# One block-triangular inverse in a chunked scan: 128-row products on the full TensorE array against 64-row block products, with the products grouped by array shape

## The chip, the cores and the metric

The kernel runs on one core of a Trainium2 chip. The metric is the device time of one execution in microseconds (us), here the median of three runs. Beside the time there is one profiled execution; its trace records each instruction of TensorE (matmuls as PE, weight loads as PEld), VectorE (DVE), ScalarE (ACT), GpSimd (POOL) and the DMA queues. Durations below are us unless marked otherwise.

## The reference

Two model blocks run one after another over 1024 tokens of width 1024. The part that the change touches most is the scan of the first block, a delta-rule recurrence over 16 heads of width 64, once forward and once backward:

```python
def rwkv7_scan(r, w, k, v, kk, a, S0, reverse):
    ...
    def step(S, inp):
        w_t, k_t, v_t, kk_t, b_t = inp[:5]
        sa = jnp.einsum('bhvk,bhk->bhv', S, kk_t)
        S = (S * w_t[:, :, None, :] - sa[..., None] * b_t[:, :, None, :]
             + v_t[..., None] * k_t[:, :, None, :])
        o = jnp.einsum('bhvk,bhk->bhv', S, inp[5]) if with_out else None
        return S, o
```

The outputs of both directions are added, normalized per head, scaled and shifted, a bonus is added and the sum is multiplied by a gate. The second block has differential attention with four heads of width 128, beside it a gated linear recurrence; their eight 128-row results are concatenated and multiplied by `w_out`:

```python
attn = rms_norm_2(attn, subln_w[l]) * (1.0 - lambda_init)
...
x = x + jnp.concatenate([attn, y], axis=-1) @ w_out[l]
```

## The kernel before

**The scan's units.** `rwkv` (line 923) cuts the 1280 tokens (256 of context, 1024 of the sequence) into ten tiles of 128. A unit is one pair of heads `i` (8 of them) and one pair of tiles `n` (5; `n` = 0 is the context, which has no output), so there are 40. In each unit both directions are done, set `x` = 0 forward and `x` = 1 backward, and each set holds four 128 x 128 problems `q` (two heads, two tiles). All work is written out by hand, one order for each engine; the engines meet by semaphores that the class `Marks` counts. In the table of names, `F` marks belong to the front of a unit (worked on during the unit before it), `L` marks to its levels, `B` marks to its back.

**The inverse.** With a chunk of 128 tokens the recurrence becomes a triangular system, (I + A) Y = R. Its inverse is built by doubling: `Y0` holds the inverses of the 2 x 2 diagonal blocks, and each level m = 1 to 6 doubles the size of the blocks. A level has three products of four 128 x 128 x 128 matmuls per set, written by the helper `quad`: `g` makes G from `Mr` and X into PSUM bank 0, VectorE (`join`) multiplies it by a mask `lev{m}` into SBUF; `x_next` makes the new X from Y and G in bank 1, `y_next` the new Y from G and Y in bank 2, and ScalarE (`x_out`, `y_out`) copies both to SBUF. `levels` (line 1280) gives TensorE's order: g of set 0, y of set 1 of the level before, g of set 1, x and y of set 0, x of set 1. Operands are of type fp32r; those of the rest of the scan are fp32, where each matmul stands twice in the trace. Each set has four PSUM banks of its own.

**The rest of a unit.** After the levels TensorE turns the next unit's keys and values (`turn_kv`, `turn_ab`), interleaved with the last y of both sets; `solve` multiplies the inverse by the right-hand sides `Rr`, `product` and `refine` do one step of refinement. Between them stand `gram_b` and `gram_k` of the next unit, products of 64 rows with the head's two halves h = 0, 1 in the two row halves of the array. `passing` makes the matrices that carry the state over a tile; `start` of the next unit transposes `Y0` to X (line 1244) and makes `MakV` (line 1247); at last `state` (line 1328) makes for each tile k and set x the new state (lines 1344, 1346, 1348) and, for n > 0, the output (lines 1353, 1355, 1357). Of these, 1344, 1346, 1353 and 1355 use all 128 rows and one column half; 1348 and 1357 are the 64 x 64 products with the carried state `S`.

```python
for x in range(2):
    if nxt:
        gram_b(*nxt, x)
    product(i, n, x)
refine(i, n, 0)
if nxt:
    gram_k(*nxt, 0)
    gram_k(*nxt, 1)
refine(i, n, 1)
for x in range(2):
    passing(i, n, x)
    if nxt:
        start(*nxt, x)
for k in range(2):
    for x in range(2):
        state(i, n, x, k)
```

**The tail.** Each pair's output is normalized by steps that sit between levels of the next pair's units: `center`, `spread`, `normal`, `affine` on VectorE, `square` and `finish` (bonus, gate) on GpSimd, `tail` (Ln, Exp) on ScalarE. For the last pair they stand alone after the last unit, and the next stage, `retention`, starts when all engines are through.

**Attention and what follows.** `attend` (line 2408) writes each head's result from `out` to the DRAM tensor `cat` by GpSimd's queue and waits for the stores at its end. `ring` is a pair of weight buffers in SBUF; `attend` loads the first two chunks of `w_out` into them. `out_up` reads `cat` back by SP's queue into `raw`, two buffers, in the order k = 0 to 3, splits each into a high and a low part (`cut.hi` on ScalarE, `cut.lo` on VectorE), loads `xb` (4 MB) on the same queue and multiplies. For the first chunk TensorE goes k by k.

Of the kernel before, what the change touches and what calls it, by code (L numbers as in the profile page):

```python
# [16 lines left out]
F32R = mybir.dt.float32r  # L17
# [846 lines left out]
class Marks:  # L864
# [23 lines left out]
    def wait(self, eng, i, name):  # L888
# [6 lines left out]
     "row", "rest"] + [f"lev{m}" for m in range(7)])}  # L895


def constants():
# [8 lines left out]
    for m in range(7):  # L907
        t[f"lev{m}"] = 1.0 * (p == f) - 1.0 * ((p >> (m + 1) == f >> (m + 1)) & (p >> m != f >> m))
# [14 lines left out]
def rwkv(nc, G, proj, Xd, oa, v_tok, rope):  # L923
# [15 lines left out]
    with nc.cleanup_on_exit(), ExitStack() as ctx:  # L939
# [23 lines left out]
        X = [sb(f"X{x}", [P, 4, P], F32R) for x in range(2)]  # L963
        Y0 = [sb(f"Y0{x}", [P, 4, P], F32R) for x in range(2)]
        Y = [sb(f"Y{x}", [P, 4, P], F32R) for x in range(2)]
        Gs = [sb(f"G{x}", [P, 4, P], F32R) for x in range(2)]
# [13 lines left out]
        spare = lambda h: bank(h, 3)  # L980

# [4 lines left out]
        def front_names(n):  # L986
            xs = n > 0
            return {"pe": ["T1", "T0", "gB", "gK", "XT", "MakV"], "act": ["Ktok", "Vtok", "Atok", "Btok", "X0", "AMv"],
                    "dve": ["tri", "MrbT", "MakT", "MrkT"] if xs else ["tri", "MakT"], "pool": ["Y0", "Mr", "AMr"]}

        def level_names(n):
            xy = sum(([f"X{m}", f"Y{m}"] if m < last else [f"Y{m}"] for m in lev), [])
            return {"pe": sum(([f"G{m}", f"X{m}", f"Y{m}"] if m < last else [f"G{m}", f"Y{m}"] for m in lev), []),
                    "act": xy, "dve": [f"G{m}" for m in lev]}
# [26 lines left out]
        with nc.Block() as block:  # L1021
            @block.sync
            def _(sp):
# [20 lines left out]
                def store(i):  # L1044
                    pool_t.wait(sp, i, "o4")
                    sp.dma_start(oa[i], o[i % 2][:]).then_inc(stored, 16)
                load(0)
# [11 lines left out]
                store(HP - 1)  # L1059
                sp.wait_ge(stored, 16 * HP)  # L1060

            @block.gpsimd
            def _(pool):
                tt, ts = nc.gpsimd.tensor_tensor, nc.gpsimd.tensor_scalar

                def front(i, n):
                    e = par_of(i, n)
                    for x in range(2):
                        F[x]["dve"].wait(pool, i, f"{n}.tri")
                        F[x]["pool"].done(tt(Y0[x][:], tri[x][e][:], rep(K("lev0"), 4), ALU.mult), f"{n}.Y0")  # L1070
# [17 lines left out]
                pool.wait_ge(set_up, 8)  # L1088
# [8 lines left out]
                square(HP - 1)  # L1097
                finish(HP - 1)

            @block.scalar  # L1100
            def _(act):
# [20 lines left out]
                def start_out(i, n, x):  # L1122
                    e = par_of(i, n)
                    F[x]["pe"].wait(act, i, f"{n}.XT")
                    F[x]["act"].done(A(X[x][:], heads(x, 1), ACT.Copy), f"{n}.X0")
                    F[x]["pe"].wait(act, i, f"{n}.MakV")
                    F[x]["act"].done(A(AM[x][e][:, :, 1], bank(x, 0)[:, 0:256].rearrange("p (q c) -> p q c", q=4), ACT.Copy), f"{n}.AMv")

                def x_out(i, n, x, m):
                    L[x]["pe"].wait(act, i, f"{n}.X{m}")  # L1130
                    L[x]["act"].done(A(X[x][:], heads(x, 1), ACT.Copy), f"{n}.X{m}")  # L1131

                def y_out(i, n, x, m):
                    L[x]["pe"].wait(act, i, f"{n}.Y{m}")
                    L[x]["act"].done(A(Y[x][:], heads(x, 2), ACT.Copy), f"{n}.Y{m}")  # L1135
# [15 lines left out]
                for i, n in UNITS_B:  # L1151
# [18 lines left out]
                    if n in (1, 2):  # L1170
                        for x in range(2):
                            out(i, n, x)
                tail(HP - 1)

            @block.tensor
            def _(pe):
# [62 lines left out]
                def start(i, n, x):  # L1239
# [3 lines left out]
                    for q in range(4):  # L1243
                        mm = mmul(bank(x, 1)[:, q * P:(q + 1) * P], Y0[x][:, q], ident_r[:], start=True, stop=True)
                    F[x]["pe"].done(mm, f"{n}.XT")
                    for q in range(4):
                        mm = mmul(bank(x, 0)[:, q * 64:(q + 1) * 64], MakT[x][:, q], KV[x][e][:, 1, q], start=True, stop=True)
# [7 lines left out]

                def g(i, n, x, m):
# [5 lines left out]
                    L[x]["pe"].done(quad(bank(x, 0), Mr[x], X[x]), f"{n}.G{m}")  # L1262

                def x_next(i, n, x, m):
# [3 lines left out]
                    L[x]["pe"].done(quad(bank(x, 1), Y0[x] if m == 1 else Y[x], Gs[x]), f"{n}.X{m}")  # L1268

                def y_next(i, n, x, m):  # L1270
                    i_, n_ = before(i, n)
                    if m == 1 and i_ >= 0:
                        B[x]["dve"].wait(pe, i_, f"{n_}.S1" if n_ < 4 else f"{n_}.S0")
# [3 lines left out]
                    L[x]["pe"].done(quad(bank(x, 2), Gs[x], Y0[x] if m == 1 else Y[x]), f"{n}.Y{m}")  # L1277
# [50 lines left out]
                def state(i, n, x, k):  # L1328
                    e = par_of(i, n)
                    t = TILES[x][2 * n + k] - at(x, n)  # L1330
                    s = (2 * n + k) % 2
                    half = lambda h: slice(64 * h, 64 * h + 64)
# [1967 lines left out]
```

## Time and profile before

| | |
|---|---|
| runs | 4991.71, 4992.29, 4998.8 us; median 4992.29 |
| the profiled execution | 4996.18 us, its span 4994.4 |
| TensorE, matmuls | 4816.6 us (96% of the span), 28888 |
| TensorE, weight loads | 3877.0 us (78%) |
| VectorE | 2559.7 us (51%) |
| ScalarE | 1870.5 us (37%) |
| GpSimd | 437.3 us (9%) |
| the scan's units | from 1387 to 2862 us of the span |
| mean granted clock of TensorE | 0.977 |

The span runs from the first to the last instruction of the trace. The time of matmuls is the union of their records, each of which holds the latency of the array as well as its own columns, so a busy PE is not yet a full one; the starts of matmuls and weight loads show the pace. A granted clock of 1.00 is 2.4 GHz, 0.50 is 1.2 GHz.

### The profile page before, as it was taken

How to read it: one execution, taken by the hardware profiler on the slowest of the kernel's cores; microseconds unless marked ns; L12 is line 12 of the kernel's file. 1: busy time of each engine (PE TensorE's matmuls, PEld its weight loads, DVE VectorE, ACT ScalarE, POOL GpSimd, SP SyncE). 2: the span in 40 equal slices, each digit the busy share in tenths (PEclk: the TensorE clock that was granted, in tenths of full speed). 3: DMA queues.
4: the chain of work that ended last, by engine and by line, in shares of the span. 5: the costliest groups of instructions: out<-in, count | busy, mean ns of one | idle time of the engine just before them, and what ended most of it. 6: DMA issues, size and time to landing. Idle time of an engine off the chain costs nothing. (4 is left out here: it accounts for less than half of the span.)

```text
span 4994.4 us, 68841 instructions
## 1 busy us (share of the span) xinstructions
PE 4816.6 (96%) x28888; PEld 3877.0 (78%) x28888; DVE 2559.7 (51%) x3696; ACT 1870.5 (37%) x3155; POOL 437.3 (9%) x352
## 2 busy tenths in 40 slices
PE   8999999999999999999999969899999879999999
PEld 5888877878988888888888734478778557888887
DVE  3344554546344554554555467554543655555553
ACT  3244434444244544545455433421233653111111
POOL 0000000000022232222322200000000000000000
PEclk9999999999989999999999989999999889999999
DMA  5333343434311011011010144242220021122222
GB/s 198 120 137 138 143 146 139 144 139 161 106 71 47 14 59 46 14 59 46 22 51 1 43 130 159 96 156 96 90 80 29 27 85 62 74 76 72 85 102 93
DMA packets 149506, 444.02 MB, mean 89 GB/s; under 512 B 16448, under 2 KB 46400, under 8 KB 131920
## 3 DMA queue, kind: packets, MB, share of 16 engines
q1 hardware_dynamic: 133856, 385.03, 21.7%
q0 software_dynamic: 9584, 33.63, 1.9%
q10 hardware_dynamic: 5760, 20.97, 1.1%
q8 instruction: 230, 3.77, 0.3%
q14 instruction: 76, 0.62, 0.0%
HBM read 295.91 MB, written 142.61 MB: 88 GB/s over the span
## 5 line engine op out<-in xcount | busy, mean ns | idle before, releaser
L172 PE MATMUL pr_ps<-uhl,w_split 128*128 128x512 f32 (+1 forms) x1520 | 586.2, 386 | 3.1 <-DVE w_split L144 2.2
L176 PE MATMUL pr_ps<-uhl,w_split 128*128 128x512 f32 (+1 forms) x1520 | 571.1, 376 | 0.0
L175 PE MATMUL pr_ps<-uhl,w_split 128*128 128x512 f32 (+1 forms) x1520 | 570.6, 375 | 0.0
L1452 DVE TENSOR_TENSOR b_G<-b_ps,cst 128x512 fp32r<-128x512 f32 x480 | 328.3, 691 | 336.5 <-PE b_ps L1253 335.2
L137 ACT ACTIVATE w_split<-share 128x2048 fp32r<-128x2048 f32 x64 | 122.6, 1915 | 689.3 <-DVE ou_vc L3128 270.8
L172 PEld LDWEIGHTS pr_ps<-uhl,w_split 128*128 128x128 f32 x1520 | 286.7, 189 | 81.6 <-issue 29.2
L1131 ACT ACTIVATE b_X<-b_ps 128x512 fp32r<-128x512 f32 x400 | 240.2, 600 | 242.5 <-PE b_ps L1253 242.5
L175 PEld LDWEIGHTS pr_ps<-uhl,w_split 128*128 128x128 f32 x1520 | 286.9, 189 | 56.0 <-issue 5.8
L176 PEld LDWEIGHTS pr_ps<-uhl,w_split 128*128 128x128 f32 x1520 | 286.5, 189 | 52.7
L1253 PE MATMUL b_ps<-b_G,b_Y 128*128 128x128 f32 x1920 | 313.6, 286 | 13.3 <-DVE b_G L1452 13.2
L1135 ACT ACTIVATE b_Y<-b_ps 128x512 fp32r<-128x512 f32 x480 | 286.6, 597 | 88.5 <-PE b_ps L1253 88.5
L1253 PE MATMUL b_ps<-b_X,b_Mr 128*128 128x128 f32 x1920 | 305.2, 286 | 0.0
L1253 PE MATMUL b_ps<-b_Y,b_G 128*128 128x128 f32 x1920 | 300.7, 280 | 0.3 <-DVE b_G L1452 0.3
L172 PE MATMUL ou_ps<-ou_a,w_split 128*128 128x512 f32 x704 | 276.4, 393 | 14.5 <-DVE ou_a L1995 14.5
L1253 PEld LDWEIGHTS b_ps<-b_G,b_Y 128*128 128x128 f32 x1920 | 255.5, 193 | 33.0 <-DVE b_G L1452 18.6
L1070 POOL TENSOR_TENSOR b_Y<-b_tri,cst 128x512 fp32r<-128x512 f32 x80 | 101.9, 1274 | 2034.0 <-DVE b_tri L1439 2034.0
L175 PE MATMUL ou_ps<-ou_a,w_split 128*128 128x512 f32 x704 | 274.6, 390 | 0.0
L176 PE MATMUL ou_ps<-ou_a,w_split 128*128 128x512 f32 x704 | 274.5, 390 | 0.0
L172 PE MATMUL mx_ps<-mx_a,w_split 128*128 128x512 f32 x640 | 258.3, 404 | 16.3 <-DVE w_split L156 16.3
L1253 PEld LDWEIGHTS b_ps<-b_X,b_Mr 128*128 128x128 f32 x1920 | 254.5, 194 | 13.5 <-issue 12.0
L1253 PEld LDWEIGHTS b_ps<-b_Y,b_G 128*128 128x128 f32 x1920 | 258.2, 195 | 0.4 <-DVE b_G L1452 0.4
L745 DVE COPY pr_stage<-pr_ps 128x256 f32<-128x256 f32 (+1 forms) x92 | 49.7, 540 | 401.8 <-PE pr_ps L176 401.7
(470 smaller groups left out, 10284.8 us busy)
## 6 DMA issues: line engine op xcount, KB each, us to landing
w_ring<-in_w_in SPq DMA_DIRECT2D x41, 1024.0 KB, 5.2
proj<-pr_stage SPq DMA_DIRECT2D x160, 256.0 KB, 2.0
share<-in_w_up SPq DMA_DIRECT2D x24, 1024.0 KB, 4.7
ar<-share SPq DMA_DIRECT2D x32, 512.0 KB, 2.8
b_AR<-ar SPq DMA_DIRECT2D x16, 1024.0 KB, 11.9
pr_raw<-proj SPq DMA_DIRECT2D x48, 256.5 KB, 3.4
ada<-in_ada_w SPq DMA_DIRECT2D x24, 512.0 KB, 5.7
ff<-ou_vc ACTq DMA_DIRECT2D x24, 512.0 KB, 2.6
```

The source lines that it names most:

```text
L137: self.nc.scalar.activation(self.hl[:, n % NBUF, 0], raw, ACT.Copy).then_inc(self.hi_done, 1)
L172: mm = nc.tensor.matmul(dst, a[0], b[0], start=start, stop=False)
L175: nc.tensor.matmul(dst, a[0], b[1], start=False, stop=False)
L176: return nc.tensor.matmul(dst, a[1], b[0], start=False, stop=stop)
L745: V.tensor_copy(dst, src).then_inc(taken[1], 1)
L1070: F[x]["pool"].done(tt(Y0[x][:], tri[x][e][:], rep(K("lev0"), 4), ALU.mult), f"{n}.Y0")
L1131: L[x]["act"].done(A(X[x][:], heads(x, 1), ACT.Copy), f"{n}.X{m}")
L1135: L[x]["act"].done(A(Y[x][:], heads(x, 2), ACT.Copy), f"{n}.Y{m}")
L1253: mm = mmul(bk[:, q * P:(q + 1) * P], lhsT[:, q], rhs[:, q], start=True, stop=True)
L1452: L[x]["dve"].done(V.tensor_tensor(Gs[x][:], heads(x, 0), rep(K(f"lev{m}"), 4), ALU.mult), f"{n}.G{m}")
```

## The change

**Levels.** Levels 1 to 5 never mix the two 64-row halves of a chunk, so they are now done on the two diagonal 64 x 64 blocks alone. Each product becomes eight matmuls with 64 rows, 64 columns of weights and 64 moved columns, alternately in the lower and the upper row half of the array; all results lie on partitions 0 to 63, block 0 in one PSUM bank and block 1 in another. ScalarE and VectorE take each result in two instructions of 64 partitions x 256 elements, which write partitions 0 to 63 and 64 to 127. G and X now share banks 0 and 1 of a set, and the y results of both sets share the two banks 2, so y of one set waits until the other's was copied. The sixth level makes only the off-diagonal corner: four matmuls for g, four for y, one eviction each. The transposes of `Y0` in `start` become block products too, and GpSimd makes `Y0` in two halves with a wait between them.

```diff
+                def blocks(at_, lhsT, rhs):
+                    for q in range(4):
+                        for b in range(2):
+                            mm = mmul(at_(b)[:, q], lhsT(b)[:, q], rhs(b)[:, q], start=True, stop=True)
+                    return mm
...
-                    L[x]["pe"].done(quad(bank(x, 0), Mr[x], X[x]), f"{n}.G{m}")
+                    if m < last:
+                        mm = blocks(lambda b: g_at(x, b), lambda b: Mr[x][rows(b), :, rows(b)], lambda b: X[x][rows(b)])
+                    else:
+                        mm = corner(g_at(x, 0), Mr[x][rows(src[x]), :, rows(dst[x])], X[x][rows(src[x])])
+                    L[x]["pe"].done(mm, f"{n}.G{m}")
...
+                    if x == 1 and m < last:
+                        L[0]["act"].wait(pe, i, f"{n}.Y{m}")
+                    if x == 0 and m > 1:
+                        L[1]["act"].wait(pe, i, f"{n}.Y{m - 1}")
...
                 def x_out(i, n, x, m):
                     L[x]["pe"].wait(act, i, f"{n}.X{m}")
-                    L[x]["act"].done(A(X[x][:], heads(x, 1), ACT.Copy), f"{n}.X{m}")
+                    for b, name in enumerate((f"X{m}a", f"X{m}")):
+                        L[x]["act"].done(A(X[x][rows(b)], x_at(x, b), ACT.Copy), f"{n}.{name}")
...
                     L[x]["pe"].wait(dve, i, f"{n}.G{m}")
-                    L[x]["dve"].done(V.tensor_tensor(Gs[x][:], heads(x, 0), rep(K(f"lev{m}"), 4), ALU.mult), f"{n}.G{m}")
+                    if m == last:
+                        L[x]["dve"].done(V.tensor_scalar(Gb[x][rows(dst[x])], g_at(x, 0), -1.0, None, ALU.mult), f"{n}.G{m}")
+                    else:
+                        for b, name in enumerate((f"G{m}a", f"G{m}")):
+                            L[x]["dve"].done(V.tensor_tensor(Gb[x][rows(b)], g_at(x, b), rep(K(f"lev{m}")[0:64, 0:64], 4), ALU.mult), f"{n}.{name}")
```

**Order.** The products of a kind stand together: both `gram_b`, both `product`, both `gram_k`, both `refine`, both `start`, both `passing`. `state` is cut in four, and for each tile all local products come first, then those with the carried state. VectorE's masks follow in the same order. The first local product also waits for the next unit's `AMv`, since `MakV` now goes to bank 2.

```diff
+                    if nxt:
+                        gram_b(*nxt, 0)
+                        gram_b(*nxt, 1)
+                    product(i, n, 0)
+                    product(i, n, 1)
                     if nxt:
                         gram_k(*nxt, 0)
                         gram_k(*nxt, 1)
+                    refine(i, n, 0)
                     refine(i, n, 1)
+                    if nxt:
+                        start(*nxt, 0)
+                        start(*nxt, 1)
+                    passing(i, n, 0)
+                    passing(i, n, 1)
                     for k in range(2):
-                        for x in range(2):
-                            state(i, n, x, k)
+                        states(i, n, k)
...
+                def states(i, n, k):
+                    for step, needed in ((state_local, passes(n, k)), (out_local, n), (state_carried, passes(n, k)), (out_carried, n)):
+                        if needed:
+                            for x in range(2):
+                                step(i, n, x, k)
```

**The last pair's tail.** Its square goes from GpSimd to ScalarE, its scale, shift, bonus and gate to VectorE, the gate in two halves that are stored one by one.

**After attention.** `out` now lies in the second buffer of `ring`. Heads 0 and 1 are stored to `cat` as before; heads 2 and 3 stay in SBUF, where `out_up` reads them first. The second chunk of `w_out` can therefore be loaded only later.

```diff
-                for k in range(HK):
-                    if k >= 2:
-                        cut.wait(sp, k - 1)
+                for k in range(2):
                     sp.dma_start(raw[:, k % 2], cat[:, k]).then_inc(raw_in[k % 2], 16)
                 sp.dma_start(xb[:], x2).then_inc(init_in, 16)
+                cut.wait(sp, 2)
+                ring.load(sp, w_o[1], 0, 0, 1, split=True)
...
+        kept, ORDER = heads_kept(ring), [2, 3, 0, 1]
```

## Rows read from the trace of the kernel before

**Rows 1.** The page, costliest groups: busy us, mean ns, idle before, releaser.
```profile
L1452 DVE TENSOR_TENSOR b_G<-b_ps,cst 128x512 fp32r<-128x512 f32 x480 | 328.3, 691 | 336.5 <-PE b_ps L1253 335.2
```

**Rows 2.** Windows; per engine busy us (count), granted clock, DMA share, GB/s.
```profile
1730.22:1745.80 15.58, 15.24 (x130) 15.01 (x128) 7.94 (x12) 10.57 (x20) 0.00 (x0) 1.00 0.00 1
1712.05:1723.84 11.79, 11.79 (x98) 9.54 (x97) 8.82 (x18) 3.02 (x7) 6.92 (x5) 1.00 0.00 1
1723.84:1730.22 6.38, 6.38 (x97) 4.47 (x96) 1.46 (x5) 0.38 (x1) 1.49 (x1) 1.00 0.01 3
...
2850.00:2852.00 2.00, 2.00 (x11) 2.00 (x11) 0.69 (x1) 1.55 (x2) 0.00 (x0) 0.50 0.00 0
...
1386.00:1414.60 28.60, 28.60 (x136) 28.48 (x135) 7.61 (x11) 12.59 (x22) 3.25 (x3) 0.50 0.37 152
```

**Rows 3.** Order of time, one level: start, us, engine, line, out<-in, count.
```profile
1736.84 0.62 PE L1253 MATMUL b_ps<-b_X,b_Mr 128*128 128x128 f32 x4
1737.34 0.66 PE L1253 MATMUL b_ps<-b_G,b_Y 128*128 128x128 f32 x4
...
1739.67 0.66 PE L1253 MATMUL b_ps<-b_X,b_Mr 128*128 128x128 f32 x4
```

**Rows 4.** Order of time, first X of a unit whose first G starts at 1730.22.
```profile
1731.67 0.66 PE L1253 MATMUL b_ps<-b_G,b_Y 128*128 128x128 f32 x4 [0.34 <-DVE b_G L1452]
```

**Rows 5.** Order of time, both `gram_k` with the next product, in two units.
```profile
1716.75 2.00 PE L1226 MATMUL b_ps<-b_AR,b_Kt 64*128 64x256 f32 x16
...
1718.68 0.66 PE L1253 MATMUL b_ps<-b_G,b_Y 128*128 128x128 f32 x4
...
1753.48 0.97 PEld L1226 LDWEIGHTS b_ps<-share 64*128 64x128 f32 x16
...
1754.57 0.52 PEld L1253 LDWEIGHTS b_ps<-b_G,b_Y 128*128 128x128 f32 x4
```

**Rows 6.** Order of time, state products of one tile and set, TensorE alone.
```profile
1723.84 0.34 PE L1344 MATMUL b_ps<-b_KV 128*64 128x64 f32 x4
...
1724.00 0.29 PE L1346 MATMUL b_ps<-b_WN,b_MB 128*64 128x64 f32 x4
...
1724.22 0.33 PE L1348 MATMUL b_ps<-b_S,b_QT 64*64 64x64 f32 x4
...
1724.48 0.44 PE L1353 MATMUL b_ps<-b_MrkT,b_KV 128*64 128x128 f32 x4
...
1724.75 0.39 PE L1355 MATMUL b_ps<-b_MB,b_WN 128*64 128x128 f32 x4
```

**Rows 7.** Order of time, two 256-element instructions in a row, ScalarE and VectorE.
```profile
1711.26 0.42 ACT L1119 ACTIVATE b_AM<-b_ps 128x256 f32<-128x256 f32 x1
1711.53 0.43 ACT L1120 ACTIVATE b_MB<-b_ps 128x256 f32<-128x256 f32 x1
...
1717.21 0.41 DVE L1460 TENSOR_TENSOR b_WN<-b_C,b_ps 128x256 f32<-128x256 f32 x1
1717.54 0.41 DVE L1461 SCALAR_TENSOR_TENSOR b_WN<-b_ps,b_C 128x256 f32<-128x256 f32 x1
...
1721.66 0.38 ACT L1127 ACTIVATE b_AM<-b_ps 128x256 f32<-128x256 f32 x1 [0.29 <-PE b_ps L1247]
```

**Rows 8.** Order of time, finish of the last pair; one of two GpSimd steps.
```profile
2875.51 1.23 DVE L1422 TENSOR_TENSOR b_o<-b_o,b_osq 128x1024 f32<-128x1024 f32 x1 [3.49 <-ACT b_osq L1108]
...
2877.67 2.34 POOL L1085 TENSOR_TENSOR b_o<-b_o,b_bonv 128x1024 f32<-128x1024 f32 x1 [10.58 <-DVE b_o L1427]
```

**Rows 9.** Order of time after attention; last row: landing of xb's load.
```profile
4085.16 0.53 POOL L2466 DMA_DIRECT2D cat_d<-at_out  x1 [7.39 <-ACT at_out L2601]
...
4089.63 1.91 ACT L153 ACTIVATE w_split<-share 128x2048 fp32r<-128x2048 f32 x1 [4.76 <-PEq L2416]
...
4095.56 0.76 PE L172 MATMUL ou_ps<-ou_a,w_split 128*128 128x512 f32 x1 [11.99 <-DVE ou_a L1995]
...
DMA to landing us min/median/max: 14.8/14.8/14.8
```

More of the change, by code:

```diff
@@ L894 @@
     ["ident", "ident64", "heads64", "after", "from", "before", "upto", "chunk", "rot", "ahead", "behind", "up", "down",
-     "row", "rest"] + [f"lev{m}" for m in range(7)])}
+     "row", "rest"] + [f"lev{m}" for m in range(6)])}
 def constants():
@@ L1172, in _ @@
                             out(i, n, x)
+                dve_t.wait(act, HP - 1, "omu")
+                pool_t.done(A(osq[:], o[(HP - 1) % 2][:], ACT.Square), "osq")
                 tail(HP - 1)
@@ L1272, in y_next @@
                     if m == 1 and i_ >= 0:
-                        B[x]["dve"].wait(pe, i_, f"{n_}.S1" if n_ < 4 else f"{n_}.S0")
+                        for z in range(2):
+                            B[z]["dve"].wait(pe, i_, f"{n_}.S1" if n_ < 4 else f"{n_}.S0")
                     if m == last:
@@ L1326, in passing @@
                     B[x]["pe"].done(mm, f"{n}.GQ")
[L1328 to L1332, printed above, removed]
+                half = lambda h: slice(64 * h, 64 * h + 64)
+                tile = lambda n, x, k: TILES[x][2 * n + k] - at(x, n)
+                passes = lambda n, k: not (n == 4 and k == 1)
+                z_of = lambda n, x, k, h: bank(x, 2)[half(h), tile(n, x, k) * 64:tile(n, x, k) * 64 + 64]
@@ new lines, in state_carried, with out_carried @@
+                def state_carried(i, n, x, k):
+                    s = (2 * n + k) % 2
+                    B[x]["dve"].wait(pe, i, f"{n}.QT")
+                    if k == 0 and n == 0:
+                        pe.wait_ge(s_zero[x], i + 1)
+                    for h in range(2):
+                        mm = mmul(z_of(n, x, k, h), QT[x][half(h), tile(n, x, k)], S[x][half(h), s], start=False, stop=True)
+                    B[x]["pe"].done(mm, f"{n}.Z{k}")
+                def out_carried(i, n, x, k):
+                    s = (2 * n + k) % 2
+                    if not passes(n, k):
+                        B[x]["dve"].wait(pe, i, f"{n}.S0")
+                    for h in range(2):
+                        mm = mmul(o_of(n, x, k, h), S[x][half(h), s], GT[x][half(h), tile(n, x, k)], start=False, stop=True)
+                    B[x]["pe"].done(mm, f"{n}.O{k}")
@@ L2453, in _ @@
                 sp.dma_start(wg[:, 1], w_x).then_inc(w_in, 16)
-                for g in range(2):
-                    ring.load(sp, w_next[g], 0, 0, g, split=True)
+                ring.load(sp, w_next[0], 0, 0, 0, split=True)
                 for k in range(RT):
```

177 lines of the change are left out of this document (106 added, 71 removed).

## The prediction

> **What bounds the kernel now.** I read the page first: TensorE is busy nearly all the time, and VectorE's most costly group in the scan idles as long as it works, always for TensorE [rows 1]. Then the table of windows over one unit (one step of the 40 in the scan, here with outputs): its levels take 15.58 us, with weight loads busy for 15.01 of them; the stretch from the first gram to the state products takes 11.79, the state products 6.38 [rows 2]. Then the order of time. In a level each of six products of four matmuls starts 0.44 to 0.50 after the one before it, and the level comes back after 2.83 us (1736.84 to 1739.67) [rows 3]: 6 x 0.44 = 2.64 and two short pauses, so TensorE sets the levels. Only the first level waits for VectorE, 1.45 us from the first G to the first X [rows 4]. Outside the levels TensorE is fed as well, but it loses time where the array's shape changes: sixteen 64-row matmuls of 256 columns cost 0.107 each (1.71) and the next 128-row one starts after 1.93, so 0.22 for the change [rows 5]. Among the state products, of the same size, it is 0.16 from one group of four to the next without a change, and 0.22 to 0.27 with one [rows 6].
>
> **The block products.** G, X and Y of levels 1 to 5 become eight matmuls of 64 rows, 64 columns of weights and 64 moved columns. No row shows them. Bounds for a product: below, the halves overlap fully, four pairs of 0.04 = 0.16; above, each costs half of a full one, 8 x 0.055 = 0.44, no gain. Between them lie groups of four 64-column matmuls, 0.16 or 0.04 each [rows 6], and the grams' weight loads: sixteen 128-column loads in the two row halves, 1.09 with the change, so about 0.06 each where a full one needs 0.11, while the 256-column matmuls ran one after another [rows 5]. I take 0.04 each, p = 0.32, the nearest row. It is complete to the waiting engine about 0.56 after its start (7 x 0.04, 0.24 for the last, as in 0.33 for four [rows 6], and 0.04).
>
> The Trainium skill, TensorEngine Tiling (Array Packing), section Key Properties, says that different tiles load weights and multiply in parallel. The grams agree for the loads and not for the multiplications (0.107 for 256 columns, in different halves); by the page p would be 0.16, which is the second rival.
>
> **The evictions double in number.** Each is now two instructions of 256 elements on 64 partitions. ScalarE starts two such 0.27 apart, and one lasts 0.38 to 0.42 [rows 7]: a pair occupies 0.54 and is seen 0.70 after its start. VectorE: 0.33 apart, 0.41 long [rows 7], 0.80 with the semaphore.
>
> The Trainium skill, VectorE: DVE Perf Modes, section Two Vector instructions with no wait between them, says that an instruction whose output starts in another quadrant than the last one's starts only when all earlier ones are finished; the halves of G write partitions 0 and 64. No row here shows such a pair. By that rule VectorE's pair would be 0.88, and the period below 2.70 in place of 2.66, or 6 us more in all.
>
> **The new level.** With TensorE at 6 x 0.32 = 1.92 and ScalarE at 4 x 0.54 = 2.16, neither is full; a ring of waits sets the pace. ScalarE takes X0, Y0, X1, Y1 in that order, so X1 starts 1.08 after X0 and is seen 0.70 later; then g of the second set issues, 0.32, and behind it in TensorE's queue the next x of the first, complete after 0.56: 1.78 + 0.32 + 0.56 = 2.66. The other ring, X0, g, VectorE, x, is 0.70 + 0.56 + 0.80 + 0.56 = 2.62. The new waits for shared banks (y of one set on the other's Y) are met inside this: y1 waits until 1.24 after X0's start, before g1 at 1.78; x behind y0 was not due. So 2.66 against 2.83, and what is late next is ScalarE's fourth-in-line X1. Stage: first X after 1.45 (0.56 + 0.80 + 0.09; now 1.45 too), four periods 10.64, then 0.56 + 1.78 and 0.16 for the corner's g: 14.6 against 15.58, so 1.0 saved. Bounds: p = 0.44 gives a period of 2.90 and a stage 0.3 longer than now; p = 0.16 gives 2.34 and 2.6 saved.
>
> **Last level and turn.** Sixth G and Y shrink from 0.44 to 0.16 each, but five changes of shape appear around the transposes (0.7), and the wait of the second solve (0.2) goes. Net 0, give or take 0.4.
>
> **Grams to passing.** Eleven changes of shape cost 1.95 in the row of 11.79 and the 0.15 ahead of it; the new order has nine at 0.13 to 0.22, 1.48. The start's four full transposes become eight block matmuls, twice 0.12 less. Saved 0.7. I followed VectorE's queue through the new order: its fourteen steps of about 0.6 end some 8 us after the first gram, passing starts at 9.3, so nothing is late. GpSimd's Y0 in two halves with a wait between is the same work, done 1.3 before the second start asks for it.
>
> **State products.** Per tile pair now 8 changes; then two. By the gaps of [rows 6] a pair of sets falls from 3.19 to 2.74. A chunk's VectorE step (seen 0.7 after the carried product) is covered by 0.96 of other products where there are outputs, so 0.95 saved in three of five units, 0.65 in the last; at n = 0, without outputs, the cover is gone and nothing is saved. Mean 0.7. The added wait, on the next unit's AMv ahead of the first local product, has all state products queued behind it; ScalarE has AMv about 0.4 to 0.8 before TensorE is through passing, so it costs nothing; were it late by one eviction, 0.4 a unit, 16 in all.
>
> **Sum.** 1.0 + 0 + 0.7 + 0.7 = 2.4 per unit, 96 us in 40. Against it: the 28 tail steps of 0.8 to 1.3 on VectorE sat in its idle half; the new gap in a level is 0.8, so each pushes the ring by some 0.4, -10. For it: the first unit ran at the lower clock (0.50, 1.2 GHz), its levels took 28.60 [rows 2]; at that clock a ring in place of full loads is about 18, 10 less where a usual unit is 1.0 less, +9. The last pair's finish leaves GpSimd: two steps of 2.34 become two halves of VectorE, together as its 1.23, less a wider step before: +3 [rows 8]. In the second block the stage after attention no longer waits for the last head's store: it issues at 4085.16 and the next stage begins at 4089.63; of 4.5 I take 3, since the split of the weights still starts the products [rows 9]. The load of the second weight chunk moves behind xb, which takes 14.8 to land [rows 9]; products start at 4095.56 and need the chunk some 23 us later, so it stays hidden by about 4; if not, 4 to 6 us are lost. Other parts of that edit (two cat loads less) cost nothing, as TensorE never waited for them. Together 101.
>
> The profiled execution took 4996.18 with a span of 4994.4; the median is 4992.29. I subtract from the median: 4891.
>
> **Rivals.**
> 1. *ScalarE does its halves one after another* (output in the other half of the partitions): a pair is 2 x 0.38 and seen after 0.81, X1 starts 1.52 after X0, period 1.52 + 0.81 + 0.32 + 0.56 = 3.21, stage 17.5 against 15.58. With 1.4 saved elsewhere a unit loses 0.5; all in all 4997, 4975 to 5040 over p. For it: nothing here shows ScalarE changing partitions. Against it: the 0.27 held between different tiles.
> 2. *The row halves overlap in the array*, p = 0.16: four rings of 2.34, 4.0 saved per unit: 4825. Against it the grams.
> 3. *The clock falls in the levels*, the slower case. Every wait there becomes part of each level. After pauses of 0.2 to 0.4 in the last unit the clock was 0.50 at 2850 to 2852 [rows 2]. At 1.2 GHz p is about 0.6, the ring 3.4, the levels 3.5 longer and 2.5 more until the clock returns behind them, as in the first unit: 6 per unit, 240 in all, 5130. It turns the result round if more than four in ten units are hit. Against it: the states, of just such small matmuls, ran at 1.00 [rows 2].
> 4. *The change doesn't do what it says*: products at p = 0.44. The levels gain nothing, the order's 1.4 stays: 4941. It is in the forecast's range.
>
> **How the numbers follow.** Forecast 0.50 (4850 to 4945), rival 2 0.13, rival 1 0.25 (0.06 faster, 0.08 same, 0.11 slower), rival 3 0.07, a smaller gain of 10 to 50 us 0.05. The measurement tells about 0.2%, 10 us, from no change. Faster 0.74, same 0.08, slower 0.18. For eight in ten the range reaches from inside rival 2 to most of rival 1: 4835 to 5015.
>
> **What would show it.** Level period 2.66; block products at 0.32; ScalarE's halves 0.27 apart (0.38: rival 1); changes of shape; states 5.4 in place of 6.38; the clock at 1.00 all through the levels; no wait for w_split in the last stage. It would be wrong at its root if ScalarE became full in the levels.

## The result, and the profile after

| | before | changed | ratio, 95% interval |
|---|---|---|---|
| time, us (median) | 4994.0 | 5214.7 | 1.044 (1.042 to 1.046) |
| span of the profiled execution | 4994.4 | 5212.8 | |
| the scan's units in it | 1386 to 2862 | 1387 to 3097 | |
| mean granted clock, whole span | 0.977 | 0.885 | |

Both kernels were timed beside each other, four executions each. The kernel became 221 us slower; forecast was 4891, range 4835 to 5015. The loss lies in the scan, which takes 1710 us in place of 1476; the rest of the kernel is some 15 us shorter. The first thing to look at is the line of the page with the granted clock, in 40 slices of the span of the changed kernel. Slices 11 to 24 hold the scan; before, its slices were all 9 but one.

```profile
PEclk8999999999867677676776769999999989999999
```

The windows of the changed kernel say the same in us (stretch, then busy us and count for TensorE, its loads, VectorE, ScalarE and GpSimd, then the granted clock, the DMA share and GB/s):

```profile
1387.00:3097.00 1710.00, 1573.65 (x18617) 1327.60 (x18618) 774.11 (x1780) 902.94 (x2370) 394.20 (x338) 0.70 0.09 33
...
1716.90:1734.00 17.10, 15.36 (x236) 13.09 (x235) 9.87 (x24) 5.24 (x15) 6.46 (x6) 1.00 0.01 1
1734.00:1757.90 23.90, 22.47 (x236) 19.45 (x238) 7.03 (x17) 17.00 (x46) 0.00 (x0) 0.50 0.01 2
1757.90:1774.90 17.00, 15.86 (x232) 13.51 (x228) 11.67 (x28) 2.90 (x8) 8.79 (x8) 1.00 0.01 2
1774.90:1802.20 27.30, 25.53 (x271) 22.39 (x268) 8.97 (x20) 18.67 (x51) 1.83 (x3) 0.50 0.00 1
...
1767.60:1772.20 4.60, 4.60 (x100) 3.86 (x94) 1.71 (x8) 0.00 (x0) 0.78 (x1) 1.00 0.01 4
```

In every unit of some 43 us (37 before) the clock falls to 0.50 soon after the levels begin (a unit's first G is at 1729.67 and at 1772.20) and in most units comes back only 24 to 27 us later, well behind them (in one of five 20 us): the turn, the solve and a gram run at half clock too. Where before 0.50 stood in the scan at its two ends alone [rows 2], it now stands in 1010 us of it. The last row is the state products: 4.60 in place of 6.38 [rows 2], and at 1.00.

On the page, the group that answers to [rows 1], and the two of ScalarE beside it:

```profile
L1529 DVE TENSOR_TENSOR b_Gb<-b_ps,cst 64x256 fp32r<-64x256 f32 x800 | 333.2, 417 | 310.3 <-PE b_ps L1283 296.3
...
L1147 ACT ACTIVATE b_X<-b_ps 64x256 fp32r<-64x256 f32 x800 | 301.5, 377 | 233.3 <-PE b_ps L1283 218.1
...
L1156 ACT ACTIVATE b_Yb<-b_ps 64x256 fp32r<-64x256 f32 x640 | 241.3, 377 | 41.2 <-PE b_ps L1283 25.5
```

And a level of the changed kernel in order of time, at half clock (start, us, engine, line; compare [rows 3]):

```profile
1779.37 0.78 ACT L1147 ACTIVATE b_X<-b_ps 64x256 fp32r<-64x256 f32 x2
...
1780.17 0.78 ACT L1156 ACTIVATE b_Yb<-b_ps 64x256 fp32r<-64x256 f32 x2
1780.20 0.64 PE L1283 MATMUL b_ps<-b_X,b_Mr 64*64 64x64 f32 x8 [0.17 <-ACT b_X L1147]
1780.65 0.61 PE L1283 MATMUL b_ps<-b_Gb,b_Yb 64*64 64x64 f32 x8
...
1780.88 0.87 DVE L1529 TENSOR_TENSOR b_Gb<-b_ps,cst 64x256 fp32r<-64x256 f32 x2 [0.66 <-PE b_ps L1283]
...
1781.31 0.78 ACT L1147 ACTIVATE b_X<-b_ps 64x256 fp32r<-64x256 f32 x2 [0.36 <-PE b_ps L1283]
...
1782.92 0.78 ACT L1147 ACTIVATE b_X<-b_ps 64x256 fp32r<-64x256 f32 x2
...
1783.75 0.64 PE L1283 MATMUL b_ps<-b_X,b_Mr 64*64 64x64 f32 x8 [0.17 <-ACT b_X L1147]
```

The G at 1780.20 has waited for the second set's X, evicted from 1779.37; the one after it in the same place is at 1783.75, so a level takes 3.55 (2.83 before). Its ring: two pairs of halves on ScalarE at 0.80 each (1781.31 to 1782.92: 1.61), seen after 0.83, G 0.45, X complete 0.66: 3.55. Two things are new in it. A pair of halves on ScalarE takes 0.80, not 0.54, and one on VectorE 0.87. And at half clock a block product occupies TensorE for 0.45.

At full clock a block product is cheaper than forecast. Sixteen matmuls (two products) take 0.65 with the last one's end and eight take 0.42, so a product occupies TensorE for 0.23:

```profile
1772.20 0.65 PE L1283 MATMUL b_ps<-b_X,b_Mr 64*64 64x64 f32 x16
...
1773.76 0.42 PE L1283 MATMUL b_ps<-b_Gb,b_Y 64*64 64x64 f32 x8 [0.90 <-DVE b_Gb L1529]
...
1774.22 0.78 ACT L1147 ACTIVATE b_X<-b_ps 64x256 fp32r<-64x256 f32 x2 [7.47 <-PE b_ps L1283]
```

X is complete to ScalarE after 0.46. From the second set's X to the G that waits for it there are 0.83 at full clock as well:

```profile
1733.13 0.78 ACT L1147 ACTIVATE b_X<-b_ps 64x256 fp32r<-64x256 f32 x2
...
1733.96 0.64 PE L1283 MATMUL b_ps<-b_X,b_Mr 64*64 64x64 f32 x8 [0.29 <-ACT b_X L1147]
```

So at full clock the ring would be 1.60 + 0.83 + 0.23 + 0.46 = 3.12, in place of 2.66 as forecast. That is an estimate from these rows.

### The profile page after: what moved, and what is told of

The parts are those of the page before. It is cut to its first block and busy times, and to the rows that moved or that the text cites. A ratio compares the mean times of both kernels' runs of the same rounds, so it can differ in the third digit from the quotient of the medians.

```text
span 5212.8 us, 80517 instructions
## 1 busy us (share of the span) xinstructions
PE 4927.2 (95%) x34008; PEld 3917.0 (75%) x34008; DVE 2595.6 (50%) x4100; ACT 2043.0 (39%) x4036; POOL 444.3 (9%) x427
## 5 line engine op out<-in xcount | busy, mean ns | idle before, releaser
L1529 DVE TENSOR_TENSOR b_Gb<-b_ps,cst 64x256 fp32r<-64x256 f32 x800 | 333.2, 417 | 310.3 <-PE b_ps L1283 296.3
L1147 ACT ACTIVATE b_X<-b_ps 64x256 fp32r<-64x256 f32 x800 | 301.5, 377 | 233.3 <-PE b_ps L1283 218.1
L1085 POOL TENSOR_TENSOR b_Y<-b_tri,cst 64x256 fp32r<-64x256 f32 x160 | 115.7, 723 | 2270.2 <-DVE b_tri L1512 2264.0
L172 PE MATMUL mx_ps<-mx_a,w_split 128*128 128x512 f32 x640 | 259.3, 405 | 15.8 <-DVE w_split L156 15.8
L1156 ACT ACTIVATE b_Yb<-b_ps 64x256 fp32r<-64x256 f32 x640 | 241.3, 377 | 41.2 <-PE b_ps L1283 25.5
L175 PE MATMUL mx_ps<-mx_a,w_split 128*128 128x512 f32 x640 | 254.1, 397 | 0.0
L176 PE MATMUL mx_ps<-mx_a,w_split 128*128 128x512 f32 x640 | 254.0, 397 | 0.0
L1283 PE MATMUL b_ps<-b_X,b_Mr 64*64 64x64 f32 x3200 | 213.2, 269 | 27.0 <-ACT b_X L1147 26.3
L651 ACT ACTIVATE pr_stage<-pr_ps 128x256 f32<-128x256 f32 (+1 forms) x92 | 43.9, 477 | 484.8 <-PE pr_ps L176 480.9
L1283 PEld LDWEIGHTS b_ps<-b_X,b_Mr 64*64 64x64 f32 x3200 | 174.2, 187 | 69.3 <-ACT b_X L1147 46.2
L175 PE MATMUL ou_ps<-ou_ext,w_split 128*128 128x512 f32 x576 | 224.1, 389 | 0.0
```

The costliest lines, as they stand in the source:

```text
L172: mm = nc.tensor.matmul(dst, a[0], b[0], start=start, stop=False)
L175: nc.tensor.matmul(dst, a[0], b[1], start=False, stop=False)
L176: return nc.tensor.matmul(dst, a[1], b[0], start=False, stop=stop)
L651: A(dst, src, ACT.Copy).then_inc(taken[0], 1)
L1085: F[x]["pool"].done(tt(Y0[x][rows(b)], tri[x][e][rows(b), :, rows(b)], rep(K("lev0")[rows(b), 0:64], 4), ALU.mult), f"{n}.{name}")
L1147: L[x]["act"].done(A(X[x][rows(b)], x_at(x, b), ACT.Copy), f"{n}.{name}")
```

## The experiments

Two theories stood against each other from the start: the half clock makes the loss (rival 3), or the halved evictions make it by themselves (rival 1). Times of before beside the runs are 4994 to 4997; intervals of the ratios are 0.0009 to 0.002 wide on either side. e9 and e12 are medians of two executions, the others of four or more.

| run | what it is | us | ratio to before | clock, 1700 to 2000 |
|---|---|---|---|---|
| e1 | levels as before, all else changed | 4903.9 | 0.982 | 1.00 |
| e2 | + one matmul nobody needs per product | 5224.5 | 1.046 | 1.00 |
| e3 | two passes, one eviction per product | 4916.8 | 0.985 | 1.00 |
| e4 | two passes, evictions in halves | 5066.7 | 1.015 | 1.00 |
| e5 | Y three times, single pass | 5382.9 | 1.078 | 0.72 |
| e6 | the same, Y's halves swapped | 5387.8 | 1.079 | 0.70 |
| e7 | X in two passes, one eviction | 4980.0 | 0.997 | 0.97 |
| e8 | X and G so | 4910.1 | 0.983 | 0.99 |
| e9 | each product twice, single pass | 5413.2 | 1.084 | 0.70 |
| e10 | e4, Y's halves swapped | 5024.1 | 1.006 | 1.00 |
| e11 | before, with the edit after attention | 4986.7 | 0.998 | |
| e12 | each product three times, single pass | 5279.7 | 1.057 | 0.94 |

**e1: the levels back, the rest kept.** `blocks` and `corner` are `quad` again, X, Y and G are evicted whole.

```
-                        mm = blocks(lambda b: g_at(x, b), lambda b: Mr[x][rows(b), :, rows(b)], lambda b: X[x][rows(b)])
...
+                    L[x]["pe"].done(quad(bank(x, 0), Mr[x], X[x]), f"{n}.G{m}")
...
-                    for b, name in enumerate((f"X{m}a", f"X{m}")):
-                        L[x]["act"].done(A(X[x][rows(b)], x_at(x, b), ACT.Copy), f"{n}.{name}")
+                    L[x]["act"].done(A(X[x][:], heads(x, 1), ACT.Copy), f"{n}.X{m}")
```

> The changed kernel with its five levels (and the sixth, and the start's transposes) put back to products of all 128 rows with one eviction each; the order of grams, products and states, the last pair's finish and the stage after attention stay as changed. Theory (the whole loss lies in the levels): the clock stays at 1.00 in the scan, levels at a period of 2.83, states 4.6 to 5.4 in place of 6.38, grams to passing 0.7 shorter; 1.4 to 2.5 us a unit, and 6 to 12 outside: 4885 to 4930. Rival (the new order of states and grams itself lets the clock fall or costs waits): 4990 or more, with stretches of the scan at 0.50.

Measured: 4903.9, 90 less than before and 311 less than the changed kernel. So the loss lies in the levels, and all else of the change is a gain of 90 us, where some 60 were forecast. This is the fastest kernel of the study. Rows of it, in order of time, of a unit with outputs: first gram, first state products, next unit's first G.

```profile
1836.73 2.14 PE L1237 MATMUL b_ps<-b_AR,share 64*128 64x256 f32 x16
...
1847.77 0.28 PE L1367 MATMUL b_ps<-b_KV 128*64 128x64 f32 x4
1847.88 0.29 PE L1369 MATMUL b_ps<-b_WN,b_MB 128*64 128x64 f32 x4
1848.00 0.29 PE L1367 MATMUL b_ps<-b_KV 128*64 128x64 f32 x4
...
1852.37 1.11 PE L1264 MATMUL b_ps<-b_X,b_Mr 128*128 128x128 f32 x8
```

Grams to passing take 11.04 in place of 11.79: 0.75 less, though the start's transposes are the old full ones here. The state products take 4.60 in place of 6.38: 1.8 less where 0.95 was forecast. A group of four with 64 columns takes 0.11 to 0.12 when its neighbours have the same shape, not the 0.16 of [rows 6], which held a change of shape.

**e2: keep TensorE busy.** One matmul of 128 rows by 64 columns, 128 moved, into the unused upper half of a bank, behind each product.

```
+                def keep(x, b):
+                    mmul(ps[64:128, 4 * x + b, 0:P], Mr[x][:, 0, 0:64].bitcast(F32), Mr[x][:, 1].bitcast(F32), start=True, stop=True)
```

> The changed kernel with one more matmul behind each g, x and y of the levels (128 rows, 64 columns of weights, 128 moved columns of plain float32), whose output nobody reads and for which nobody waits: some 1500 us-neutral additions of work on TensorE, about 0.1 us each at full clock. Theory A (the lower clock makes the loss, and it falls since TensorE is idle and half empty in the pauses of a level): the clock is 1.00 or near it, the level period 3.2 to 3.5, and the time falls to 4980 to 5060 although more is computed. Theory B (the evictions set the time by themselves and the clock is only its witness): 5215 or more, the clock as it may be.

The clock did stay at 1.00, but the time is one that was expected under theory B. It doesn't speak for B either, for the filler was too dear. In order of time on TensorE:

```profile
1760.01 0.42 PE L1283 MATMUL b_ps<-b_X,b_Mr 64*64 64x64 f32 x8
...
1760.36 0.43 PE L1292 MATMUL b_ps<-b_Mr 128*64 128x128 f32 x2
...
1760.72 0.42 PE L1283 MATMUL b_ps<-b_Gb,b_Yb 64*64 64x64 f32 x8
```

A product and its filler take 0.71: 0.23 and 0.11 of work and 0.37 for two changes, from 64 rows to 128 and back and, since the filler is plain float32, of the operands' kind as well. Six of them are 4.3 a level; TensorE had become the bound. The run is inconclusive as to the price of the clock. It does show that halved evictions alone don't lower the clock: they are the changed kernel's here, and it is 1.00.

**e4: the same products in two passes.** Plain float32 operands make each block product two passes of the array, sixteen records in place of eight. Order, evictions and waits are the changed kernel's.

```
-                            mm = mmul(at_(b)[:, q], lhsT(b)[:, q], rhs(b)[:, q], start=True, stop=True)
+                            mm = mmul(at_(b)[:, q], lhsT(b)[:, q].bitcast(F32), rhs(b)[:, q].bitcast(F32), start=True, stop=True)
```

> The changed kernel with its block products in plain float32, two passes each in place of one; order, evictions and waits as they are. TensorE has about twice the work in the levels. Theory A (clock): it stays at 1.00, ring 3.2 plus twice 0.2 = 3.6, levels about 19.5: 5040 to 5100, faster than the 5215 of the changed kernel with more work. Theory B (the clock doesn't matter, or it falls all the same): 5260 or more.

Measured: 5066.7, clock 1.00. The matmuls of TensorE's block products are doubled and the kernel is 148 us faster than the changed one. Theory A stands. A window of e4, then VectorE's evictions of two G's of one set, one level apart:

```profile
1700.00:2000.00 300.00, 285.17 (x5667) 246.75 (x5664) 145.77 (x343) 171.77 (x457) 71.72 (x61) 1.00 0.12 45
```

```profile
1833.31 0.87 DVE L1529 TENSOR_TENSOR b_Gb<-b_ps,cst 64x256 fp32r<-64x256 f32 x2
...
1836.93 0.87 DVE L1529 TENSOR_TENSOR b_Gb<-b_ps,cst 64x256 fp32r<-64x256 f32 x2 [1.25 <-PE b_ps L1283]
```

The period is 3.62, as worked out ahead. With single passes it would be 3.12 at this clock, 0.50 x 4 x 40 = 80 us less: 4987 for the changed kernel without its lower clock. Two more places would gain by single passes. The first level, from the first G to the next level's, takes 2.68 in the changed kernel at full clock (1729.67 to 1732.35) and 3.37 in e4; a set of transposes with what follows takes 1.39 in the one and 1.65 in the other:

```profile
1720.95 0.42 PE L1268 MATMUL b_ps<-b_ident_r,b_Y 64*64 64x64 f32 x8
...
1722.34 0.42 PE L1268 MATMUL b_ps<-b_ident_r,b_Y 64*64 64x64 f32 x8
```

```profile
1852.29 0.68 PE L1268 MATMUL b_ps<-b_ident_r,b_Y 64*64 64x64 f32 x16
...
1853.94 0.68 PE L1268 MATMUL b_ps<-b_ident_r,b_Y 64*64 64x64 f32 x16
```

The first pair is of the changed kernel, the second of e4. These are 0.7 and 0.5 a unit, 48 us in 40, which brings the estimate down to 4939. So the clock costs between 228 and 276 us, and the rest, 35 to 83 against the 4904 of e1, lies in the halves. No run gave either figure directly.

**e3: one eviction in place of two.** The products are e4's, but block b's results go to partitions 64b of the same columns, so that X, G and all but the last Y are evicted by one instruction of 128 x 256.

```
+        both = lambda x, k: ps[:, 4 * x + k, 0:256].rearrange("p (q f) -> p q f", q=4)
...
-                    for b, name in enumerate((f"X{m}a", f"X{m}")):
-                        L[x]["act"].done(A(X[x][rows(b)], x_at(x, b), ACT.Copy), f"{n}.{name}")
+                    L[x]["act"].done(A(X[x][:], both(x, 1), ACT.Copy), f"{n}.X{m}")
```

> Of the changed kernel: block b's products go to the partitions 64b to 64b+63 of one bank, so that X, Y and G are evicted by one instruction of 128 partitions x 256 elements in place of two of 64 x 256; for that the block products are in plain float32 (two passes each). The two last Y halves stay two. Theory: the evictions in halves set the ring of 3.2; with one each the period is set by TensorE (6 products of about 0.4 = 2.4) and the clock stays at 1.00: levels 13 to 14 in place of 15.6, some 4 a unit less than before with the order's part: 4800 to 4870. Rival 1 (the clock falls for block products however they are fed): period 2.9 to 3.2 at 0.50, 5000 to 5100. Rival 2 (float32 passes of 64x64 cost 0.07 each, p = 1.1): period over 3.5, over 5050 at clock 1.00.

Measured: 4916.8, clock 1.00; the theory's mechanism, but not its size (4800 to 4870 expected). VectorE's evictions of two G's of one set in e3, one level apart:

```profile
1818.08 0.42 DVE L1522 TENSOR_TENSOR b_Gb<-b_ps,cst 128x256 fp32r<-128x256 f32 x1 [0.31 <-PE b_ps L1282]
...
1820.88 0.42 DVE L1522 TENSOR_TENSOR b_Gb<-b_ps,cst 128x256 fp32r<-128x256 f32 x1 [1.44 <-PE b_ps L1282]
```

The period is 2.80: six products of 0.467, not 0.4 as expected, TensorE full, the evictions out of the way. Against e4 it is 150 us: the halves are a bound of their own. e3 differs from e4 in the evictions and, with them, in that the sets no longer wait for each other's banks. In e4 that wait isn't what sets the level: y of the second set waits 0.16 for such a bank at 1833.28, but the G behind it waits until 1834.09 for X anyway. Two-pass block products are as dear as full ones of one pass (2.80 against 2.83), so there is no gain over e1.

**e5 and e6: more of the single-pass products.** Y's eight matmuls are issued three times into the same place; in e6 ScalarE takes Y's upper half first.

```
+                        for again in range(3):
+                            mm = blocks(lambda b: y_at(x, b), lambda b: Gb[x][rows(b)], lambda b: was[rows(b)])
...
-                        for b, name in enumerate((f"Y{m}a", f"Y{m}")):
+                        for b, name in ((1, f"Y{m}a"), (0, f"Y{m}")):
```

> The changed kernel with each Y product of the levels issued three times into the same place (the same single-pass 64-row matmuls, no other shape, no longer wait for X and G; only the third is signalled). 10 block products a level for TensorE in place of 6, 2.2 us of about 3.2. Clock theory: it stays at 1.00, the level period is what the halves on ScalarE set, 3.2; against the kernel with all block products in two passes (5067, period 3.62) it saves 0.4 x 4 x 40 = 64: about 5000, 215 less than the changed kernel with 640 us/1000 of added work in each level pair. That difference is then the price of the clock, and 5000 against 4904 that of the halves. Theory B (idle time is not what lowers the clock): it falls as before, 5215 or more.

> The same (Y three times) with ScalarE taking Y's halves in the other order, upper first: the order of partitions is then low, high, high, low. Theory (a change of output partition is what makes a half start 0.40 after the last instead of 0.27): X, Y, X, Y take 1.34 to 1.40 in place of 1.60 and X of the second set starts 0.12 to 0.2 earlier: period 3.0 to 3.1, 20 to 30 us less than Y three times in the old order. Rival (halves of 64 partitions follow each other at 0.40 whatever they write): no difference beyond 10 us.

(What e5 adds is four block products a level; the "640 us/1000" is a slip.) Measured: 5382.9 and 5387.8, clock 0.72 and 0.70. My clock theory in this form fell: ten products a level in place of six, of the same kind, didn't hold the clock. At half clock ten products of 0.47 are 4.7 a level, TensorE is the bound, and swapping the halves could change little, so e6's total is silent on its question.

**e9 and e12: as many passes, of the other kind.** Each product issued two or three times.

```
+                    for again in range(2):
+                        for q in range(4):
+                            for b in range(2):
+                                mm = mmul(at_(b)[:, q], lhsT(b)[:, q], rhs(b)[:, q], start=True, stop=True)
```

> The changed kernel with every block product of the levels (G, X and Y) issued twice into the same place, single-pass: the same number of 64x64x64 passes, in the same order and at the same places, as the kernel with two-pass products (5067, clock 1.00, period 3.62). Theory A (what lowers the clock is how many passes TensorE makes and how long it idles between them): the same as that one, clock 1.00, 5050 to 5080. Theory B (a single pass of the short float counts for less than one of the two passes of float32, however densely they come): the clock falls in the levels, a product twice is then 0.9, six of them 5.5 a level, 5500 to 5650.

> The same three times over: at full clock 18 x 0.22 = 4.0 a level, so TensorE would never pause in the levels. Theory A (pauses lower the clock): clock 1.00, period 4.0, 5120 to 5200. Theory B (the kind of product lowers it, pause or no pause): the clock falls, a level takes 8 us, 5950 to 6200.

Measured: 5413.2 and 5279.7. e9 makes the same number of 64x64x64 passes in the same places as e4 and its clock falls unit after unit, where e4's stays. A window of e9, then two of e12, a stretch at either level:

```profile
1700.00:2000.00 300.00, 294.93 (x4324) 267.54 (x4324) 123.12 (x277) 144.12 (x372) 67.45 (x57) 0.70 0.09 31
```

```profile
1848.80:1882.90 34.10, 33.01 (x452) 30.87 (x453) 8.56 (x18) 13.27 (x36) 3.59 (x4) 0.50 0.02 7
1882.90:2074.00 191.10, 187.55 (x4301) 171.73 (x4301) 89.07 (x207) 100.03 (x262) 46.94 (x40) 1.00 0.11 41
```

With three times the products TensorE never pauses between them in the levels at full clock (period 4.20, 18 products of 0.233), and the clock holds for 191 us, but not for good: 283 us of the scan are still at 0.50. Neither theory as written: e9 bears out B as to the clock (its time is below B's range), e12 lies between. Both matter, how densely the products come and of which kind they are. Single-pass products of 64 rows held the clock through most of the scan when they followed each other without a pause (e12), and not with pauses; two-pass ones held it with pauses too (e4). What the chip counts was not found.

**e7 and e8: two passes where the ring needs them.** In e7 X alone is two-pass and evicted whole, in e8 G as well.

```
-        x_at = lambda x, b: low(x, b, 256)
+        x_both = lambda x: ps[:, 4 * x + 1, 256:512].rearrange("p (q f) -> p q f", q=4)
+        x_at = lambda x, b: x_both(x)[rows(b)]
```

> The changed kernel with X alone in plain float32 (two passes), block b's X on the partitions 64b of one bank and evicted by one instruction of 128 x 256; G and Y stay single-pass with two evictions of 64 x 256. TensorE has 0.22 + 0.47 + 0.22 per set, 1.9 a level; ScalarE 0.27 + 0.80 a set. Ring: the second set's X starts 1.07 after the first's, is seen 0.45 later, then g 0.22 and the next X product 0.6: 2.35. Theory: the clock stays at 1.00 (8 passes in 2.35 us, as the two-pass kernel's 12 in 3.62), levels 2.35: 4820 to 4860. Rival: the clock falls in parts of the units: 4950 to 5100.

> The same with G in two passes and one eviction too; only Y is left in halves. TensorE 0.47 + 0.47 + 0.22 a set, 2.33 a level, which then is the period: TensorE full, clock 1.00, 4830 to 4870. Rival: the wait of one set's Y for the other's eviction makes it 2.5 to 2.8: 4870 to 4920.

Measured: 4980.0 and 4910.1, both in the range of the rival and not of the theory. e7's clock falls in five units besides the first, for 20 to 27 us each, and its ten executions scatter from 4965 to 4993; at full clock its level takes 2.96, not 2.35. e8's clock stays, but its level takes 2.85, not 2.33, and not for the rival's reason: after a unit's first level TensorE waits for no eviction there. In order of time on TensorE's loads in e8, a single-pass Y and the two-pass product behind it:

```profile
1857.18 0.31 PEld L1283 LDWEIGHTS b_ps<-b_Yb,b_Gb 64*64 64x64 f32 x8
...
1857.53 0.54 PEld L1283 LDWEIGHTS b_ps<-b_Gb,b_Yb 64*64 64x64 f32 x16
```

It takes 0.35 where 0.23 is its own, and the product ahead of it, from 1856.57, 0.61 in place of 0.47: going from one kind to the other costs 0.12 to 0.14 each way. There are four such changes a level, 0.52, which is all of 2.85 less 2.33.

**e10: the order of the halves, at full clock.** e4 with e6's swap.

> The kernel with two-pass block products (5067, clock 1.00) with ScalarE taking Y's halves upper first. In the trace of Y three times, a half that writes the same partitions as the one before starts 0.28 after it, one that changes them 0.40. Theory: X of the second set starts 1.36 after X of the first in place of 1.60, and that is in the ring: period 3.38 in place of 3.62, 0.24 x 4 x 40 = 38 less: 5025 to 5040. Rival (the ring runs through VectorE's halves or TensorE's queue): no less than 5057.

Measured: 5024.1, 43 less than e4 and 1 below the theory's range. ScalarE in e10, in order of time:

```profile
1863.27 0.78 ACT L1147 ACTIVATE b_X<-b_ps 64x256 fp32r<-64x256 f32 x2 [0.36 <-PE b_ps L1283]
1863.95 0.77 ACT L1156 ACTIVATE b_Y<-b_ps 64x256 fp32r<-64x256 f32 x2
1864.62 0.77 ACT L1147 ACTIVATE b_X<-b_ps 64x256 fp32r<-64x256 f32 x2
```

The next pair starts 0.68 behind the last in place of 0.80: a half that writes the same partitions as the one ahead starts 0.28 after it, one that goes to the others 0.40, which is when the one ahead is done. X of the second set starts 1.35 after the first's, and a level takes 3.36 (VectorE's G's at 1854.83 and 1858.19). It shows both the mechanism and that this ring sets the levels.

**e11: the edit after attention alone**, on the kernel before.

```
+    kept, ORDER = heads_kept(ring), [2, 3, 0, 1]
...
+                cut.wait(sp, 2)
+                ring.load(sp, w_o[1], 0, 0, 1, split=True)
```

> The kernel before with the edit of the stage after attention alone (heads 2 and 3 stay in the ring's buffer, the second weight chunk is loaded behind xb, no wait for the last head's store). Theory: 3 us less (0 to 4.5): 4988 to 4994 beside 4994. Rival: the later chunk is waited for, 4 to 6 us more.

Measured: 4986.7, ratio 0.9983 (0.9975 to 0.9992): 4 to 12 us less. A gain, more than the 3 forecast.

## Why the prediction was wrong, step by step

- **Block product, p.** Forecast 0.32 (0.16 to 0.44); measured 0.23 at full clock, 0.45 at half. At the pace of the grams (256 columns in 0.107 [rows 5]) eight matmuls of 64 columns are 0.21, at half that clock 0.43: they ran one after another, with their loads hidden. The Trainium skill, TensorEngine Tiling (Array Packing), section Key Properties, says that different tiles multiply in parallel, which was the forecast's 0.16; no run here shows that, and the measurement decides. The term was 0.09 too large and it was not the one that mattered.
- **The evictions.** This is the first step that failed: "a pair occupies 0.54", taken from two instructions that wrote the same partitions [rows 7]. Halves go to other partitions each time, and a pair takes 0.80 on ScalarE and 0.87 on VectorE. For VectorE the prediction had 0.88 by the Trainium skill, VectorE: DVE Perf Modes, section Two Vector instructions with no wait between them, and the trace agrees. That ScalarE does likewise was rival 1, to which I gave 0.25 with "nothing here shows ScalarE changing partitions". Rival 1's ring was 3.21; by the measured parts it is 3.12 at full clock in place of the forecast's 2.66, and longer than the 2.83 of before. By the estimate above that is 4939 to 4987 without the lower clock; the rival said 4997.
- **The clock.** This is the step that decides: the forecast had TensorE at full clock all through the levels, and it was at 0.50 in nearly all of them. Rival 3 was priced about right: "the ring 3.4, the levels 3.5 longer and 2.5 more until the clock returns", 240 in all; measured are 3.55 a level, and 228 to 276 by the estimate. Its chance, 0.07, was wrong. I set against it that the state products, "just such small matmuls", ran at 1.00 [rows 2]. They do, but they are plain float32, two passes each, and follow each other without a pause; neither holds in the levels. e9 against e4 shows that the kind matters, e5 and e9 against e12 that the pauses do. The two rivals weren't exclusive either, as the chances assumed. That the slower ring of rival 1 helps the clock to fall by its longer pauses is likely, but not shown: no run has single-pass blocks in a faster ring.
- **Levels, sum.** First G of a unit to its first solve takes 23.87 in a usual unit, 18.14 before: 5.7 more where 1.0 less was forecast. (The means over all 40 units are 24.4 and 19.0; before, the first unit alone took 32.4.)
- **The tail steps.** Forecast 10 us lost. The units that hold them, the first two of each pair of heads, take together 3.6 more than two usual ones, 3.3 before: some 2 us over the seven pairs.
- **Last level and turn.** Forecast net 0. The changed kernel's are hidden under the half clock. In e3, which has the same corner at full clock, first G to first solve takes 17.92 in a usual unit, 18.14 in e1: of the 0.22, 0.12 are the four periods. So 0.1 for the corner: right.
- **Grams to passing.** Forecast 0.7 saved, 0.75 measured in e1. That the sizes agree is luck. Of the 0.7 the order was to bring 0.47 and the transposes in blocks 0.24; e1 has the old transposes, so the order alone brought 0.75. Both transposes with `MakV` behind them take 2.77 in the changed kernel at full clock (1720.95 to 1723.72) and 2.77 in e1 (1843.65 to 1846.42): the blocks saved nothing.
- **State products.** Forecast 0.95 where there are outputs, 1.8 measured; over all five kinds of unit the stretch from the first solve to the next first G is 15.9 in e1, 17.9 before, so order and states save 2.0 a unit, 82 us, where 56 was forecast. Right in kind, too small. The added wait on AMv costs nothing, as said.
- **First unit.** Forecast 9 less; first G to first solve 23.7, 32.4 before: 8.7 less. Right. It is also the one place where the blocks gain, since all of it ran at half clock before too (e1, with the old levels, takes 31.6).
- **Last pair's finish.** Forecast 3; from the last eviction of outputs to the next stage 18.5 in place of 24.4: 5.9 less. Some 1.6 of it is luck: TensorE's means of the squares ran at half clock before (3.55) and at full clock now (1.99).
- **After attention.** Forecast 3; e11 gives 4 to 12. From the last eviction to the first product there are 6.5 us in place of 10.7.

So six terms were right in kind, three of them too small by about half, and what of them stands in e1 is worth 90 us. The two that failed, the time of a pair of evictions and the clock, stood in one place, the levels. The Trainium skill, TensorEngine Tiling (Array Packing), section PSUM Bottleneck, says that tiling speeds up TensorE but not the evacuation of PSUM, and advises to let one access cover several tiles of a bank; e3 against e4 shows it in numbers here, 150 us, and I hadn't weighed it.

## What to carry to other kernels

Before a full engine is relieved, ask what its fullness was good for: here 128-row products kept TensorE at its full clock, and blocks with half the work and pauses between them lost 311 us against e1, by the estimate 228 to 276 of them through the clock and the rest through halved evictions. A price per instruction holds only for the same pattern as its row: two evictions to the same partitions followed each other at 0.28, two to different ones at 0.40. And a change with several parts is worth taking apart: levels as before with the rest of the change is 1.8% faster than before (4904).

## What the runs showed of the hardware

- The granted clock depended on the kind of matmul, not on TensorE's busy share alone: with the same count of 64x64x64 passes a level it was 1.00 in two passes of plain float32 (e4) and 0.70 in single passes issued twice (e9). In the changed kernel it fell in each unit after pauses of TensorE of 0.2 to 0.9 between block products, and once at 0.50 it stayed there for 20 to 27 us.
- ScalarE started a 64x256 eviction 0.28 after the last one if it wrote the same 64 partitions and 0.40 if it wrote the others (e10); VectorE's pairs of halves take 0.87.
- Going from a single-pass to a two-pass product of the same shape and back cost TensorE 0.12 to 0.14 each time (e8), and changing both the rows, 64 to 128 and back, and the kind some 0.18 each time (e2).
- Block products of 64 rows in the two row halves ran one after another: eight of 64 columns took 0.23 at full clock and 0.45 at half.
